# Later staging, earlier loads and postponed row sums at the hand-over between two expert passes

## The reference

```
s = einsum('thpd,hpnd->thpn', q, sub_keys)            # q = h @ w_q, two halves of 128 keys
sv, si = top_k(s, 16)
cand = sv[:, :, 0, :, None] + sv[:, :, 1, None, :]     # 256 pairs, 16 best of them
eidx = expert numbers of the best pairs                # 128 a token
g = softmax(their scores)
a = gelu(einsum('ted,td->te', u_tab[eidx], h))
y = einsum('te,ted->td', g * a, v_tab[eidx])
x = x + g2 * y
```

## Time and profile before

| | us |
|---|---|
| runs | 3293.95, 3284.65, 3279.32 |
| median | 3284.65 |
| the profiled execution: time | 3293.95 |
| the profiled execution: span | 3292.2 |
| its mean granted TensorE clock | 0.974 |

### The profile page before, as it was taken

One profiled execution on the slowest core, in us unless ns is written; L12 is line 12 of the kernel. 1 busy time (PEld: TensorE's weight loads), 2 busy tenths in 40 slices (PEclk: granted clock), 3 DMA queues, 4 the chain that ended last, 5 costly groups with the idle time before them and its releaser, 6 DMA issues.

```text
span 3292.2 us, 42610 instructions
## 1 busy us (share of the span) xinstructions
PE 3141.6 (95%) x16753; PEld 2702.1 (82%) x16753; DVE 2039.4 (62%) x3710; ACT 1272.3 (39%) x2160; POOL 793.4 (24%) x495
## 2 busy tenths in 40 slices
PE   6999999999999999999998999999999997999999
PEld 3777898978888888888887678999999996887877
DVE  5684656554332464333367555978978766787877
ACT  5363434434232334332334332335444453333332
POOL 0000101000000020000001200576776764454342
PEclk8998999989999999999998799999999998999999
DMA  2222212133333323332222022478888889999997
GB/s 85 87 68 77 67 56 71 52 109 93 99 96 96 115 84 103 96 96 96 81 88 67 1 65 78 160 249 297 297 280 328 283 320 346 343 335 341 334 337 261
DMA packets 231080, 538.17 MB, mean 163 GB/s; under 512 B 22545, under 2 KB 88337, under 8 KB 227809
## 3 DMA queue, kind: packets, MB, share of 16 engines
q1 hardware_dynamic: 193440, 399.09, 37.0%
q0 software_dynamic: 37440, 136.36, 11.3%
HBM read 482.92 MB, written 52.46 MB: 163 GB/s over the span
## 4 chain that ended last, share of the span: by engine, by line
PE 67%; DVE 15%; DMA 10%; POOL 3%; issue 2%; ACT 2%; SPq 1%; DVEq 0%; ACTq 0%
PE bank L343 22%; PE bank L346 15%; PE bank L2231 11%; DMA gl<-acts 7%; DVE vsl L2709 3%; DMA eu<-in_peer_u 3%; DVE y_row L2276 3%; PE bank L1000 2%; POOL etl L2219 2%; PE bank L2390 2%; PE bank L1010 2%; PE bank L1805 2%; PE bank L964 2%; DVE coefl L2729 1%; PE bank L952 1%
## 5 line engine op out<-in xcount | busy, mean ns | idle before, releaser
L293 DVE TENSOR_TENSOR wl<-raw,wh 128x1024 fp32r<-128x1024 f32 (+3 forms) x239 | 294.0, 1233 | 638.9 <-ACT wh L278 638.8
L278 ACT CAST wh<-raw 128x1024 fp32r<-128x1024 f32 (+3 forms) x239 | 247.2, 1037 | 652.3 <-PE bank L343 367.7
L2219 POOL TENSOR_TENSOR etl<-eu,eth 128x1024 fp32r<-128x1024 f32 x128 | 317.7, 2484 | 416.8 <-ACT eth L2215 415.8
L2231 PE MATMUL bank<-peerhh,eth 128*128 128x384 f32 x1024 | 348.9, 341 | 19.3 <-POOL etl L2219 15.9
L2231 PE MATMUL bank<-peerhl,eth 128*128 128x384 f32 x1024 | 342.9, 335 | 0.0
L2231 PE MATMUL bank<-peerhh,etl 128*128 128x384 f32 x1024 | 342.9, 335 | 0.0
L2662 PE MATMUL bank<-vsh,coefh 128*128 128x512 f32 x768 | 301.3, 392 | 28.2 <-DVE coefl L2729 28.2
L2256 POOL DMA_INDIRECT taken<-in_peer_v,gb x128 | 247.3, 1932 | 290.5 <-DVE y_row L2276 284.0
L2662 PE MATMUL bank<-vsh,coefl 128*128 128x512 f32 x768 | 300.1, 391 | 0.0
L2662 PE MATMUL bank<-vsl,coefh 128*128 128x512 f32 x768 | 299.8, 390 | 0.0
L2215 ACT CAST eth<-eu 128x1024 fp32r<-128x1024 f32 x128 | 135.5, 1059 | 201.9 <-DMA eu<-in_peer_u 201.7
(11 more groups left out here) (548 smaller groups left out, 7326.7 us busy)
## 6 DMA issues: line engine op xcount, KB each, us to landing
eu<-in_peer_u SPq DMA_DIRECT2D x128, 512.0 KB, 4.7
vb<-in_peer_v SPq DMA_DIRECT2D x128, 512.0 KB, 5.1
raw<-in_ada_w SPq DMA_DIRECT2D x48, 512.0 KB, 3.9
acts<-eg SPq DMA_DIRECT2D x128, 192.0 KB, 4.1
coefs<-stage SPq DMA_DIRECT2D x24, 1024.0 KB, 7.2
gd<-coefs SPq DMA_DIRECT2D x16, 1536.0 KB, 14.7
gl<-acts SPq DMA_DIRECT2D x128, 192.0 KB, 6.5
raw<-in_ffn_w_gate SPq DMA_DIRECT2D x44, 512.0 KB, 3.6
```

The source lines that it names most:

```text
L278: act.copy(parts_of(c)[0], raw_of(c)).then_inc(*up("w rounded", c))
L293: dve.tensor_tensor(lo, raw_of(c), hi.bitcast(F32), ALU.subtract).then_inc(*up("w split", c))
L2219: pool.tensor_tensor(Et[j % 3][1], Eu[j % 2], Et[j % 3][0].bitcast(F32), ALU.subtract).then_inc(*up("u split", j))
L2231: t = pe.matmul(b, tb[un][:, k * 128:(k + 1) * 128], peer_h[hn][:, k, 1:4, :], start=k == 0 and i == 0, stop=k == 7 and i == 2)
```

## The change

- Tile 3's exp, turn and pairs stand three to four units later (`EXP_AT` 99 to 103, `TURN_AT` 102 to 105, `PAIRS_AT` 103 to 106). The table for the gathers ends at dot 119 by unit 123, so the last fetched dots come after the units.
- A part's coefficients are written by one transfer of 2 MB, at the place of the first of the two of 1 MB that stood a unit apart.
- SP goes over to the second pass at unit 124 instead of 126 (`V_AHEAD` = 4): after `ROUTED`, it issues the loads of experts 0, 1, 2 with units 124, 125, 126 between them. Within a load, `gd` comes before `vb` instead of behind it. ScalarE interleaves experts 0 to 2 and the last units in the same way.
- VectorE starts the product of expert 0 after dot 120. The last 8 dots go into experts 0 to 5. The gelu of the gathered tile comes at expert 6, its weights at expert 8, and all 128 sums are spread over experts 9 to 127 (`SUMS_AT` = 8).

```diff
-    SCORES_AT, EXP_AT, TURN_AT, PAIRS_AT = (0, 2, 16, 56), (8, 28, 65, 99), (0, 34, 71, 102), (0, 36, 74, 103)
+    SCORES_AT, EXP_AT, TURN_AT, PAIRS_AT = (0, 2, 16, 56), (8, 28, 65, 103), (0, 34, 71, 105), (0, 36, 74, 106)
-    DOTS_BY = ((8, 0), (16, 4), (28, 15), (36, 23), (53, 45), (65, 56), (74, 64), (91, 86), (100, 97), (117, 119), (121, 120),
-               (122, 124))
+    DOTS_BY = ((8, 0), (16, 4), (28, 15), (36, 23), (53, 45), (65, 56), (74, 64), (91, 86), (103, 97), (123, 119))
...
-                for half in range(2):
-                    units()
-                    on_sp.wait_ge(*at("staged", tt, part, 28))
-                    sp.dma_start(Gd[tt * 4 - 4 + part][:, 2048 * half:2048 * half + 2048],
-                                 stage[part % 2][:, 64 * half:64 * half + 64, :].rearrange("p j t -> p (j t)")).then_inc(
-                                     *up(f"coefs out {part % 2}", tt, part, by=16))
+                units()
+                on_sp.wait_ge(*at("staged", tt, part, 28))
+                sp.dma_start(Gd[tt * 4 - 4 + part], stage[part % 2].rearrange("p j t -> p (j t)")).then_inc(
+                    *up(f"coefs out {part % 2}", tt, part, by=16))
...
-    FIRST_SUMS = 4, 7
+    V_AHEAD, SUMS_AT = 4, 8
...
         def load(j):
-            if j >= 3:
-                on_sp.wait_ge(*at("v split", j - 3))
-            sp.dma_start(Vb[j % 3], Vd[:, j, :]).then_inc(*up(f"v in {j % 3}", j, by=16))
             if j % 8 == 0:
                 if j >= 16:
                     on_sp.wait_ge(*at("coef prod", j - 9))
...
+            if j >= 3:
+                on_sp.wait_ge(*at("v split", j - 3))
+            sp.dma_start(Vb[j % 3], Vd[:, j, :]).then_inc(*up(f"v in {j % 3}", j, by=16))
...
-        units.until(NJ - 2)
+        units.until(NJ - V_AHEAD)
         for what in ROUTED:
             on_sp.wait_ge(*at(*what))
-        load(0)
-        load(1)
-        units()
-        load(2)
-        units()
+        for j in range(V_AHEAD - 1):
+            load(j)
+            units()
+        units.until(NJ)
         sp_store(sp, on_sp, NJ - 1)
-        for j in range(3, NJ):
+        for j in range(V_AHEAD - 1, NJ):
             load(j)
...
-        units.until(NJ - 3)
-        on_act.wait_ge(*at("row used", 127))
-        act.activation(a_first, a_first, ACT.Gelu).then_inc(*up("first gelu"))
-        units.until(NJ - 1)
-        v_part(0)
-        units()
-        for j in range(NJ):
-            if j:
-                v_part(j)
-            coef_part(j)
+        units.until(NJ - V_AHEAD + 1)
+        for j in range(V_AHEAD - 1):
+            parts(j)
+            units()
+        for j in range(V_AHEAD - 1, NJ):
+            parts(j)
+            if j == SUMS_AT - 2:
+                on_act.wait_ge(*at("row used", 127))
+                act.activation(a_first, a_first, ACT.Gelu).then_inc(*up("first gelu"))
...
-        dots.until(128)
-        on_dve.wait_ge(*at("first gelu"))
-        on_dve.wait_ge(*at("dve step", "route", 0, "weights"))
-        dve.tensor_tensor(a_first, a_first, g_first, ALU.mult).then_inc(*up("dve step", "first weights"))
-        sums(FIRST_SUMS[0])
+        done = 0
+        dots.until(120)
+        first = dots.j
+        prod(0)
         v_rest(0)
-        sums(FIRST_SUMS[1])
-        prod(0)
...
-            sums(min(128, FIRST_SUMS[1] + (128 - FIRST_SUMS[1]) * (j + 1) // (NJ - 1)))
+            if j < SUMS_AT - 2:
+                dots.until(first + (128 - first) * (j + 1) // (SUMS_AT - 2))
+            elif j == SUMS_AT:
+                on_dve.wait_ge(*at("first gelu"))
+                on_dve.wait_ge(*at("dve step", "route", 0, "weights"))
+                dve.tensor_tensor(a_first, a_first, g_first, ALU.mult).then_inc(*up("dve step", "first weights"))
+            elif j > SUMS_AT:
+                while done < 128 * (j - SUMS_AT) // (NJ - 1 - SUMS_AT):
+                    dve_sum(dve, on_dve, done)
+                    done += 1
```

More of the change, by code:

```diff
@@ L2675, in act_experts, with parts @@
     def act_experts(act, on_act, units):
-        def v_part(j):
+        def parts(j):
             on_act.wait_ge(*at(f"v in {j % 3}", j))
@@ L2683, in v_part @@
             act.copy(Vs[j % 4][0], Vb[j % 3]).then_inc(*up("v rounded", j))
-        def coef_part(j):
             on_act.wait_ge(*at("coef prod", j))
             act.copy(Cb[j % 4][0], gl[j % 5]).then_inc(*up("coef rounded", j))
-        units.until(NJ - 3)
-        on_act.wait_ge(*at("row used", 127))
-        act.activation(a_first, a_first, ACT.Gelu).then_inc(*up("first gelu"))
-        units.until(NJ - 1)
-        v_part(0)
-        units()
-        for j in range(NJ):
-            if j:
-                v_part(j)
-            coef_part(j)
+        units.until(NJ - V_AHEAD + 1)
[7 more added lines that the diff above has]
+                act.activation(a_first, a_first, ACT.Gelu).then_inc(*up("first gelu"))
     def dve_experts(dve, on_dve, dots):
```

## The result

The kernel after takes 3299.31 us (median of 7 runs, 3293.67 to 3305.15), the kernel before, on the same chip, 3282.77 (7 runs, 3269.79 to 3293.95). The ratio is 1.0055, with a 95% interval of 1.0038 to 1.0074: 16.5 us slower. The profiled execution of after took 3298.84 us, with a span of 3297.1; that of before was the slowest of its runs. So the two profiles differ by only 4.9 us.

What follows compares the result with a forecast made beforehand. The prediction took TensorE as the floor, with VectorE and the load queue ending last in most second-pass blocks. Its terms, -4.7 + 18.2 = +13.5 us, gave 3298 us on the median, range 3279 to 3315.

Steps and rivals of the forecast that it cites:

- Writes merged: First pass: the 2 MB write delays the `eu` load behind it, exposed after tile 2's last write; 2 us, bounds 0 and 6.
- Later staging and coarser table: Tile 3 in the first pass: nothing becomes late except where `eu` cannot keep up, about 1 us lost.
- Hand-over: Between the passes: earlier second-pass loads mostly move TensorE's stall from before the experts to before unit 126; gain 4.4 us.
- First reload hidden: First eight experts: without sums, the first `gd` reload is hidden, its `gl` landing at 2771.5 instead of 2777.3.
- Sums: Experts 16 to 119: 13 more sums at 1.4 us each cost 18.2 us; bounds 0.5 and 2.0 per sum.
- Order of `gd` and `vb`: Second-pass loads: `gd` enters the queue 2.9 us earlier, but the queue is busy, so nothing is gained.
- End: End of the kernel: two more sums use up VectorE's 2.31 us wait for the first finished output; 0.
- sums absorbed: Rival for the second pass: added sums cost 0.5 us each or less, total 3280 to 3292; chance 0.22.
- Faster: Rival between the passes: the 16.7 us `coefl` wait really goes, total 3267 to 3275; chance 0.08.
- Clock dips: Rival for the second pass: 2.0 us per sum, and longer `gd` waits drop TensorE's clock; 3306 to 3312; chance 0.18.
- Worse hand-over: Rival: `eu` 126 comes at 2737 and twelve write delays leak 1 us each, +12 on top, 3310; chance 0.10.
- the rule about memory: Second pass: about 358 GB/s per core would make memory the bound, 4.14 us per expert; the prediction said the trace disagrees.

Runs made afterwards that it cites:

- e2: The kernel before with only the two 1 MB coefficient writes of a part made one of 2 MB: 3288.89 us, ratio 1.0019.
- e3: The kernel before with no sums before the first expert or in the first nine, all 128 spread over experts 9 to 127: 3291.69 us, ratio 1.0028.
- e4: The kernel before with the seven sums ahead of the first product moved, all 128 spread evenly from expert 0 on: 3285.90 us, ratio 1.0017.
- e12: The kernel before with each `gd` reload in three pieces and no sums ahead of the experts: 3268.12 us, ratio 0.9961.
- e6: The kernel after with two 1 MB writes and `vb` ahead of `gd` again: 3299.54 us, ratio 1.0034 to the kernel before.
- e9: The kernel after with only the old order, `vb` ahead of `gd`, restored: 3298.50 us, ratio 1.0063 to the kernel before.
- e7: The kernel after with `SUMS_AT` at 24 instead of 8, so 128 sums over 103 experts: 3314.71 us, ratio 1.0084 to the kernel before.
- e10: The kernel after with each `gd` reload but the first in three 512 KB pieces, issued earlier: 3271.99 us, ratio 0.9964 to the kernel before.
- e11: The kernel before with each `gd` reload in the same three pieces: 3275.54 us, ratio 0.9979.
- e8: The kernel after with 2 KB instead of 4 KB per token in the sums' gathered rows, changing the output: 3276.87 us, ratio 0.9967 to the kernel before.
- e1: The kernel before with only `gd` put ahead of `vb` within a load: 3283.02 us, ratio 1.0002.
- e5: The kernel before, unchanged, run again on the second chip for a second profile: 3291.57 us in one run.

## Why the prediction was right, and where it was not

The sum said +13.5 us and the measurement 16.5 (12.5 to 24 by its interval). The term that was to make the kernel slower, the 13 sums more in the body of the second pass, did so, at about its size. That the total came within 3 us is in part luck: the writes missed by +2, the tables by -7, the hand-over by +2, the first reload by +8 and the sums by -2, and these nearly cancel. Term by term, with the table's differences between after and before:

*Writes merged, predicted +2.* Measured about +5 to +7: e2 and the first column of the table. The 2 MB writes landed as put:

```profile
DMA to landing us min/median/max: 8.3/9.7/10.7
```

That is inside my 8 to 13. The place was right (from unit 93 to 94 after took 9.2 us, before 6.8, and over all profiles it is 2.1 us), but the other writes, put at nothing inside the pair stretches, were not fully hidden: less than 1 us each.

*Later staging and coarser table, predicted +1.* Measured -6 from unit 94 to 125 (168.1 to 162.0, and 161.3 to 165.3 in the other kernels with the new tables). I had the wrong sign. These windows of before and after show TensorE's idle time there, 7.1 us before and 0.8 after:

```profile
2549.90:2718.00 168.10, 160.96 (x1003) 159.41 (x1004) 124.51 (x187) 80.25 (x97) 114.46 (x68) 0.99 0.84 302
```

```profile
2551.70:2713.70 162.00, 161.21 (x1004) 160.49 (x1005) 116.94 (x175) 78.86 (x95) 112.08 (x64) 0.98 0.83 288
```

TensorE's waits for `etl` fell, and fewer bytes are asked for in this stretch (288 GB/s instead of 302), as the gathers of the last dots moved out of it. That these moved bytes are the cause is only argued; no run changed the tables alone.

*Hand-over, predicted -4.4.* Measured -2.5 from unit 125 to the first expert (29.4 to 26.9). The mechanism is as told: the stall moved in front of unit 126, 12.0 us, in the range of 12 to 16 given, because `eu` 126 stands behind the last write's landing and `gd`, `vb` and `gl`. Two units at the lower clock took back 2.4. What I overlooked is where the gain comes from. The old hand-over with the seven sums taken out has the first expert 22.6 to 23.1 us after unit 125 (e3, e4, e12), sooner than in any kernel with the earlier loads (26.0 to 28.7). So the sums' absence gave more than 6 us, and the rest of the new hand-over lost some 4 of it.

*First reload hidden, predicted -3.3.* This step failed. I put the landing of `gl` 8 at 2771.5, and it landed at 2772.96; but I had not asked when TensorE would want it. With its first expert at 2740.6 and 4.11 us each, expert 7 was due at 2769.3 and began at 2774.15, 4.85 us late. Experts 0 to 15 took 72.7 us instead of 68.3, and 71.6 and 72.2 in e6 and e9. In e7 expert 7 was in time, and they took 65.3; why that one escaped is not shown. So after expert 16 the kernel was level (+4.2, -6.1, -2.5 and +4.4 are 0.0), not 4.7 ahead.

*Sums, predicted +18.2.* In the pair of profiles the pass grew by 7.1 us only, but before's profiled execution was an unusually slow one. I take it here that executions of one kernel differ mostly ahead of unit 0, which is not shown. Three kernels with the pass at its floor tell what a usual run of before takes from unit 0 on: e10 is 1193.8 and 10.3 faster, e11 1198.8 and 6.8 faster, e12 1192.0 and 14.2 faster, so 1204.1, 1205.6 and 1206.2. The profiled 1216.1 is 10 to 12 above that, and after's 1223.5 is 17 to 19 above it, near the measured 16.5. That puts the sums' term at about 16 of the 16.5 (16.5, less the 0.0 up to expert 16 and 0.3 at the end), which is worked out and not seen in one profile of before; e3, where only the sums change, gives the same 16.0. For 13 sums that is 1.2 each, where I took 1.4. Blocks of eight experts, from the start of every eighth on, say about the same: in before 33.0 us with seven sums and 34.3 with eight, in after 33.7 with eight and 34.7 with nine. So my 2.0 from the landings of `gl` was too high. With ten sums (e7) a block takes 36.7, against 35.2 with nine in e6 on the same chip, so they grow dearer. What I had wrong is that a sum has a price of its own. It has none when `gd` comes in pieces (e10: 112 of them for nothing). I read the cost as that of a queue near its limit, hit by a burst: while 1.5 MB of `gd` pass, the `gl` behind it and the rows share what is left, `gl` lands 11 to 16 us after its issue in after, and VectorE has not built up that much lead. More rows mean less lead. Half the row bytes (e8) or smaller bursts (e10) both bring TensorE to its floor.

*Order of `gd` and `vb`, predicted 0:* +1.0 us from e1 and -0.3 from e9 (by the medians), nothing that their intervals can tell from 0. *End, predicted 0:* 0.3.

Of the rivals, *sums absorbed* fell: waits for `coefl` came to 21.2 us, near the 25 given and not 12. *Faster* fell with the 12.0 us wait for `etl`. *Clock dips* in the pass did not come: the granted clock was 0.99 from 2745 on. *Worse hand-over* did not come either: twelve write delays leak, but less than 1 us each, and `eu` 126 landed at 2726.38, not so late that its units began at 2737.

On the rule about memory: the Trainium skill ("Perfetto Trace Analysis", Roofline) says that 358 GB/s is a core's share only when both cores of a pair stream, and that one alone can draw more, up to about 435 by its 16 DMA engines. The trace agrees on the first half: 362 GB/s over 450 us in e10, 414 over 14 us. It does not show 435: with this mix of pieces the engines were at a share of 1.00 at 362, and in the 14 us at 1.03 with 414.

Left open: how much of its second pass a usual run of before waits. The 1205, less the other columns of before's profile and its 37.3 us behind expert 119, leaves some 428, so 4 us above the floor; e11 took 6.8 away, and e1's one profile has no wait, with a median like before's. The profiles of e6 and e7 exceed the 1205 by 23 and 38 us, their medians by 9 and 24; but against e5, the kernel before on their own chip (1214.2), it is 14 and 29, near the 11 and 28 that their ratios give.

## What to carry to other kernels

Where a bandwidth-bound pass misses its floor by a few per cent, look at the largest transfer in the queue before counting bytes: the same bytes in thirds, two to six loads earlier, gave 27 us on the kernel after and 7 on the kernel before, more than any shift of work. An edit's price measured beside such a burst (a sum: 1.2 us) is no property of the edit, so remove the burst first and then ask again what may be postponed. And a loader moved ahead of a stall only moves the stall, if it waits for the same last write: for each load ask both when it lands and when its user will want it.

## What was not expected of the hardware

- The sixteen DMA engines moved 362 GB/s over 450 us at a share of 1.00 (e10), but only 333 at 0.94 when more rows were asked for in bursts (e7).
- 1.5 MB of `gd` in pieces of 1 KB landed in 14.8 us at the median in after, in 11.4 where the gathered rows were half as wide (e8); 512 KB of it took 7.9 us (e10), more than half the time for a third of the bytes.
- The same program differs from chip to chip by 8 us, and its stages ahead of the change by up to 13 us between executions, more than most terms of this sum.
